# Sparse-attention decode on one Trainium2 core: selected keys on one DMA queue, selected values on the other

## What is computed

```python
# per batch b: 32 pages of 128 past tokens, found through page_table[b]
kc, vc = compressed_kv(dense(pool_cmp_k, kcr), dense(pool_cmp_v, vcr), ...)   # one key and value per 16 tokens
...
p_c = masked_softmax(einsum(q, kc) * sc, mask_c)                # compressed branch
score = where(valid, einsum(p_c.sum(3), overlap) + forced, NEG) # importance of blocks of 64 tokens
top_val, top_idx = top_k(score, 16)
s_s = einsum(q, ks[top_idx]) * sc;  o_s = masked_softmax(s_s) @ vs[top_idx]   # selected branch
o_w = masked_softmax(einsum(q, kw) * sc, mask_w) @ vw                         # last 512 tokens
o = g0 * o_c + g1 * o_s + g2 * o_w
y = x + gate * ((o * silu(z)) @ c_w_out)
# after it, for prompt and sample: y = rmsnorm(y) * final_norm
```

## Time and profile before

| | |
|---|---|
| median of three runs | 1283.19 us (1278.74 to 1287.04) |
| profiled execution, its own time | 1283.88 us |
| its span | 1282.2 us |
| PE busy | 1186.6 us (93%) |
| DVE, ACT, POOL busy | 485.5, 426.2, 200.0 us |
| mean granted clock of TensorE | 0.964 of full speed |
| moved by DMA | 238.77 MB, mean 186 GB/s |

### The profile page before, as it was taken

How to read it: one execution, slowest core, us unless ns; L and a number is a source line. 1 busy time by engine, 2 the same in 40 slices (tenths; PEclk the granted TensorE clock), 3 DMA queues, 4 the chain that set the end, 5 groups by cost and what they waited for, 6 DMA issues and landing times. The chain is left out here.

```text
span 1282.2 us, 25368 instructions
## 1 busy us (share of the span) xinstructions
PE 1186.6 (93%) x9191; PEld 749.0 (58%) x9191; DVE 485.5 (38%) x1491; ACT 426.2 (33%) x1080; POOL 200.0 (16%) x337
## 2 busy tenths in 40 slices
PE   4899999999999799999997999999998979889996
PEld 1677754766767457477875555555554434444455
DVE  2543033444412501022203666556565323333334
ACT  3322113233310420011011656656665223333452
POOL 0000000000000101012002222222223423434300
PEclk8899999999989899999898999999999889989998
DMA  9655543203071302125005767766676989898972
GB/s 382 250 198 197 197 164 91 119 1 132 1 271 66 144 1 73 68 74 186 3 1 207 247 219 260 263 226 224 225 244 193 343 291 310 302 311 283 344 266 75
DMA packets 96440, 238.77 MB, mean 186 GB/s; under 512 B 12602, under 2 KB 50620, under 8 KB 91836
## 3 DMA queue, kind: packets, MB, share of 16 engines
q1 hardware_dynamic: 74076, 169.14, 37.5%
q0 software_dynamic: 22240, 68.02, 15.0%
HBM read 227.57 MB, written 17.05 MB: 191 GB/s over the span
## 5 line engine op out<-in xcount | busy, mean ns | idle before, releaser
L405 PE MATMUL ps<-arena,wring 128*128 128x288 f32 x1664 | 427.3, 413 | 3.7 <-DMA wring<-in_weights 2.2
L405 PEld LDWEIGHTS ps<-arena,wring 128*128 128x128 f32 x1664 | 315.4, 192 | 102.4 <-issue 14.1
L1628 POOL DMA_DIRECT2D arena<-in_cmp_pages x128 | 70.1, 548 | 276.8 <-PE ps L1793 100.5
L414 PE MATMUL ps<-wring,arena 128*128 128x512 f32 x192 | 92.0, 614 | 7.1 <-ACT arena L1366 7.1
L1721 DVE CUSTOM_DVE_ANT_0 wring<-ps,wring 128x128 f32<-128x128 f32 (+3 forms) x128 | 57.6, 488 | 72.4 <-PE ps L1650 71.0
L2186 DVE CUSTOM_DVE_ANT_1 arena<-ps,small 128x512 f32<-128x512 f32 x64 | 44.3, 693 | 93.1 <-PE ps L2105 93.0
L2162 ACT ACTIVATE arena<-arena 128x512 f32<-128x512 f32 (+1 forms) x88 | 57.0, 648 | 67.4 <-DVE arena L2202 67.4
L1713 ACT ACTIVATE wring<-ps 128x128 f32<-128x128 f32 (+3 forms) x128 | 49.1, 436 | 86.8 <-PE ps L1673 86.8
L1699 ACT ACTIVATE wring<-wring 128x128 f32<-128x128 f32 (+3 forms) x128 | 70.7, 559 | 8.6 <-DVE wring L1721 8.5
L2173 ACT ACTIVATE arena<-ps 128x512 f32<-128x512 f32 x72 | 43.0, 598 | 87.0 <-PE ps L2126 87.0
L1786 PE MATMUL ps<-arena 128*32 128x256 f32 x1024 | 69.5, 389 | 0.0
(11 more groups left out here) (396 smaller groups left out, 1572.9 us busy)
## 6 DMA issues: line engine op xcount, KB each, us to landing
wring<-in_weights SPq DMA_DIRECT2D x27, 2048.0 KB, 11.0
arena<-in_cmp_pages SPq DMA_DIRECT2D x128, 256.0 KB, 3.4
arena<-in_cmp_pages POOLq DMA_DIRECT2D x128, 256.0 KB, 4.4
wring<-in_kv_pages SPq DMA_DIRECT2D x64, 256.0 KB, 9.3
wring<-in_kv_pages POOLq DMA_DIRECT2D x64, 256.0 KB, 6.9
arena<-in_kv_pages SPq DMA_DIRECT2D x50, 256.0 KB, 7.3
arena<-in_kv_pages POOLq DMA_DIRECT2D x50, 256.0 KB, 7.1
arena<-in_out_tiles SPq DMA_DIRECT2D x12, 512.0 KB, 7.9
```

What stands on the lines that cost most here:

```text
L405: last = pe.matmul(out[:, 0:HT], w[:, k, ct * P:ct * P + P], moving[k][:, half * HT:half * HT + HT], start=(k == 0), stop=(k == KT - 1))
L414: last = pe.matmul(main, tokens, w[:, k, :], start=(k == 0), stop=(k == KT - 1))
L1628: eng.dma_start(cring[q % CR][:, 2 * half + j, :], v["cmp_pages"][bass.ds(ids[2 * d + j], 1)] .rearrange("o p c -> (o p) c")).then_inc(c_i ...
```

## The change

- **Queues.** SP's queue brings all keys (`load_keys`), GpSimd's all values (`load_values`), one DMA of 128 rows x 256 f32 per page and kind, and one of 512 KB for each half of the window. Each kind has its own semaphores, and a key load waits for the key home alone, a value load for the value home alone. `pe_scores` waits for keys alone; `pe_values` waits for its values. Page numbers are now read per tile and queue, behind the wait, from a table in plain order.
- **Output tiles.** From n = 1 on, output tile n is loaded behind all keys of batch n.
- **Tail.** The samples' last projection is 16 matmuls of 512 columns, from weights in another order (`out_rows`), in four pairs of k that wait for one piece of the weights each. The sum of squares over k is a TENSOR_REDUCE on DVE and one matmul.
- **Prompt's masks.** `prompt_cmp_max(0)` now comes ahead of `prompt_cmp_mask(1)` on DVE.

```diff
@@ names of DV3
-        names = ["ca0", "ca1", "cm0", "cp0"]
+        names = ["ca0", "cm0", "ca1", "cp0"]
...
-        def wait_home(eng, n, i):
+        def load_keys(eng, n, i):
 
             at = n * NL + i
             if at < CR:
...
                 eng.wait_ge(pe_a, PE3["pv", U - 1])
             else:
                 eng.wait_ge(scored, (at - KR) // NL * NJ + (at - KR) % NL + 1)
+            home, done = keys_home(n, i), k_in[at % KR]
+            if i == NG:
+                eng.dma_start(home, v["win_kv"][n, :, 0:HALF]).then_inc(done, 16)
+                return
+            ids = page_ids(eng, 0, (n * NG + i) * GP)
+            for q in range(GP):
+                eng.dma_start(home[:, q * KVW:q * KVW + KVW], v["kv_pages"][bass.ds(ids[q], 1)]
+                              .rearrange("o p c -> (o p) c")[:, 0:KVW]).then_inc(done, 16)
+
+        def load_values(eng, n, i):
+
+            at = n * NL + i
+            if at < CR:
+                eng.wait_ge(pe_c, PC_["pool", NB - 1, CR + 2 + at // 2])
+            elif at < KS:
+                eng.wait_ge(pe_a, PE3["pv", U - 1])
             if KS - CR <= at < KS:
                 eng.wait_ge(dve_c, DC_["sel", NB - 1])
             if at >= KS:
                 n0, i0 = (at - KS) // NL, (at - KS) % NL
                 eng.wait_ge(valued, n0 * NJ + JS.index(i0) + 1)
-
-        def bring(eng, n, i, half, lo, cols, src):
-
-            k, vals, done = keys_home(n, i)[:, lo:lo + cols], values_home(n, i)[:, lo:lo + cols], kv_in[half][(n * NL + i) % KS]
-            if vals.offset > k.offset:
-                both = bass.AP(k.tensor, k.offset, [list(k.ap[0]), [vals.offset - k.offset, 2], [1, cols]])
-                eng.dma_start(both, src.rearrange("p (x c) -> p x c", x=2)).then_inc(done, 16)
-            else:
-                eng.dma_start(k, src[:, 0:cols]).then_inc(done, 16)
-                eng.dma_start(vals, src[:, cols:2 * cols]).then_inc(done, 16)
-
-        def load_kv(eng, half, n, pair):
-            ids = page_ids(eng, 0, ((n * (NG // 2) + pair) * 2 + half) * GP)
-            for d in range(2):
-                i = 2 * pair + d
-                wait_home(eng, n, i)
-                for j in range(2):
-                    bring(eng, n, i, half, (2 * half + j) * KVW, KVW,
-                          v["kv_pages"][bass.ds(ids[2 * d + j], 1)].rearrange("o p c -> (o p) c"))
...
+            home, done = values_home(n, i), v_in[at % KS]
+            if i == NG:
+                eng.dma_start(home, v["win_kv"][n, :, HALF:2 * HALF]).then_inc(done, 16)
+                return
+            ids = page_ids(eng, 0, (n * NG + i) * GP)
+            for q in range(GP):
+                eng.dma_start(home[:, q * KVW:q * KVW + KVW], v["kv_pages"][bass.ds(ids[q], 1)]
+                              .rearrange("o p c -> (o p) c")[:, KVW:2 * KVW]).then_inc(done, 16)
@@ pe_scores
-                pe.wait_ge(kv_in[0][(n * NL + i) % KS], kv_total[0, n, i])
-                if i < NG:
-                    pe.wait_ge(kv_in[1][(n * NL + i) % KS], kv_total[1, n, i])
+                pe.wait_ge(k_in[(n * NL + i) % KR], landed(n, i, KR))
@@ pe_values
+            if j <= NG:
+                pe.wait_ge(v_in[(n * NL + j) % KS], landed(n, j, KS))
@@ SP's program
-                    for pair in range(NG // 2):
-                        load_kv(sp, 0, n, pair)
-                        if pair == 1:
-                            sp.wait_ge(*((tile_done, n) if n else (pe_c, PC_["turn", NB - 1, 1])))
-                            sp.dma_start(lohi_[:, 0:1024], v["out_tiles"][n]).then_inc(tile_in, 16)
-                    load_window(sp, n)
+                    for i in range(NL):
+                        load_keys(sp, n, i)
+                        if n == 0 and i == 3:
+                            sp.wait_ge(pe_c, PC_["turn", NB - 1, 1])
+                            sp.dma_start(lohi_[:, 0:1024], v["out_tiles"][0]).then_inc(tile_in, 16)
+                    if n:
+                        sp.wait_ge(tile_done, n)
+                        sp.dma_start(lohi_[:, 0:1024], v["out_tiles"][n]).then_inc(tile_in, 16)
@@ GpSimd's program
-                    for pair in range(NG // 2):
-                        load_kv(pool, 1, n, pair)
+                    for i in range(NL):
+                        load_values(pool, n, i)
@@ PE, the samples' output projection and the sum of squares
-                for ct in range(4):
-                    for k in range(KT):
+                    for k in range(2 * i, 2 * i + 2):
                         for half in range(2):
-                            last = pe.matmul(ps[half * NS:half * NS + NS, 2 + half, ct * P:ct * P + P], zT[:, k, TP:NT],
-                                             last_w[4 * half + ct][:, k, :], start=(k == 0), stop=(k == KT - 1))
+                            last = pe.matmul(ps[half * NS:half * NS + NS, 2 + half, :], zT[:, k, TP:NT],
+                                             last_w[2 * i + half][:, k % 2, :], start=(k == 0), stop=(k == KT - 1))
...
-                for k in range(KT):
-                    if k == 0:
-                        pe.wait_ge(s_squares, 1)
-                    last = pe.matmul(ps[:, 4, 0:NS], ones, f_sqs[:, k, :], start=(k == 0), stop=(k == KT - 1))
-                last.then_inc(s_summed, 1)
+                pe.wait_ge(s_squares, 1)
+                pe.matmul(ps[:, 4, 0:NS], ones, s_sum, start=True, stop=True).then_inc(s_summed, 1)
@@ DVE
                 prompt_cmp_mask(dve, 0)
+                prompt_cmp_max(dve, 0)
                 prompt_cmp_mask(dve, 1)
-                prompt_cmp_max(dve, 0)
...
-                dve.tensor_tensor(f_sqs, xs, xs, ALU.mult).then_inc(s_squares, 1)
+                dve.tensor_tensor(f_sqs, xs, xs, ALU.mult)
                 dve.drain()
+                dve.tensor_reduce(s_sum, f_sqs.rearrange("p k n -> p n k"), AX.X, ALU.add).then_inc(s_squares, 1)
```

More of the change, by code:

```diff
@@ L217, in out_tiles, with out_rows @@
     return head_pairs(v["c_w_out"][0].T).T.reshape(KT, P, KT, P).transpose(2, 1, 0, 3).reshape(KT, P, KT * P)
+def out_rows(v):
+    return out_tiles(v).reshape(2, 4, P, 4, 2, P).transpose(0, 3, 2, 4, 1, 5).reshape(KT, P, KT * P)
 def narrow_weights(w):
@@ L2026, in build, with landed @@
         sums11 = sums_.rearrange("p (b c) -> p b c", b=2)
-        kv_in = [[sem(f"kv_in_{eng}{s}") for s in range(KS)] for eng in ("sp", "pool")]
-        kv_total, kv_count = {}, [[0] * KS, [0] * KS]
-        for at in range(NB * NL):
-            pieces = 1 if v_homes[at % KS].offset > k_homes[at % KR].offset else 2
-            for h in range(2):
-                kv_count[h][at % KS] += 16 * pieces * (2 if at % NL < NG else 1 - h)
-                kv_total[h, at // NL, at % NL] = kv_count[h][at % KS]
+        k_in = [sem(f"keys_in{s}") for s in range(KR)]
+        v_in = [sem(f"values_in{s}") for s in range(KS)]
+        def landed(n, i, homes):
+            at = n * NL + i
+            return sum(16 * (GP if a % NL < NG else 1) for a in range(at % homes, at + 1, homes))
         JS = list(range(NG)) + [NG + 1, NG]
@@ L2231, in build @@
         f_sqs = SS[:, 0:KT * NS].rearrange("p (k n) -> p k n", k=KT)
-        last_w = [keys_home(NB - 1, 1 + ct).rearrange("p (k c) -> p k c", k=KT) for ct in range(KT)]
-        last_in = [sem(f"last_tiles_in{i}") for i in range(4)]
+        last_w = [keys_home(NB - 1, 1 + i).rearrange("p (k c) -> p k c", k=2) for i in range(KT)]
+        last_in = [sem(f"last_rows_in{i}") for i in range(4)]
         f_squares, f_summed, f_rooted = sem("f_squares"), sem("f_summed"), sem("f_rooted")
@@ L2238, in build @@
         s_tok = SS[:, KT * NS:KT * NS + TP]
+        s_sum = SS[:, KT * NS + TP:KT * NS + TP + NS]
         def pe_out_tile(pe, n):
@@ L2294, in _ @@
                     for h in range(2):
[L2295 removed]
+                        sp.dma_start(keys_home(NB - 1, 1 + 2 * i + h), v["out_rows"][4 * h + i]).then_inc(last_in[i], 16)
                 y = v["y"].rearrange("p (k n) -> p k n", k=KT)
```

10 lines of the change are left out of this document (4 added, 6 removed).

## The result

The changed kernel takes 1273.7 us (median of 20 runs, 1266.85 to 1282.4). The kernel before took 1281.76 us in 20 runs (1276.05 to 1290.24). The ratio is 0.993, 95% interval 0.9908 to 0.9953: faster, but by 6 to 12 us where 24 were forecast. Four stretches hold this difference: 2.1 us lie ahead of 684 us, in code that was not changed (the prompt's first matmuls start anywhere from 680.5 to 690.7 us in the profiled executions of this case); 2.9 us between the prompt's first matmuls and phase 0; 8.0 us in the seven phases; 0.3 us in the tail.

The account below looks back on a forecast made before the run. The prediction took PE to be held up by SP's wait before each output tile, with SP's issuing the next bound. Gains of 3.0 (start), 20 (phases) and 0.9 (tail), 23.9 us, from 1283.9 gave 1260 us; range 1246 to 1281.

Parts of the forecast that it names:

- DMA's pace: Rival for the seven phases: DMA stays at 306 GB/s, 1280.0 us, or reaches 323 GB/s, 1266.7 us; chance 0.30.
- Its second cause: In the phases: window and output tile, issued together, still take 12 us to land and PE waits once a batch; 1280.0 us.
- PE's pace: Rival for the phases: SP's page-number blocks overlap more, so PE bounds; 32.5 us gained there, 1247.5 us in all; chance 0.13.
- SP slower than its own rows: Rival for SP's key loads: 0.75 us a step, so a batch takes 36.2 us and the kernel 1309.5 us; chance 0.12.
- The signs set down: Trace signs of being right, among them phases 1 to 6 at 29 to 30 us each and 330 to 345 GB/s.
- the chance of 0.68: Chance of a time under 1270.4 us, faster by more than 1% (13 us); within 1% had 0.20, slower 0.12.
- 29.2 us of issuing per batch: SP's queue in the phases: eight tiles of 3.52 us plus window and output tile, more than PE's 27.9 us.
- I allow one such stall per batch in six, 0.5 us a batch: SP's loads in the phases: allowance for a full queue holding a load 2.74 us; lowers the gain from 22.9 to 20 us.
- the 7.9 us of the earlier trace: Start of phase 1: time from output tile 1's issue to its landing, putting that phase's start at 1039.6 us.
- The start: Prompt's first masks on DVE: DVE goes on 3.1 us earlier and PE takes it all, 3.0 us gained.
- The tail: End of the kernel: wide matmuls gain nothing, the sum of squares on DVE brings the reciprocal earlier; 0.9 us gained.
- put at nothing: GpSimd's value loads in the phases: 28.1 us per batch, costed at nothing because its lead of over 25 us covers it.

Follow-up runs that it names:

- e1: Changed kernel with SP taking the keys' page numbers as program constants instead of reading them from the table; 1248.64 us, ratio 0.9763 to the kernel before.
- e2: Changed kernel with loads of 128 x 128 instead of 128 x 256 on both queues from the seventeenth tile on, same instructions; 1269.89 us, ratio 0.9907.
- e7: Changed kernel without the range checks of page numbers on both queues, loads still dynamic; 1251.56 us, ratio 0.9779 to the kernel before.
- e9: Changed kernel without the split (each queue brings keys and values of its pages) and without bound checks of page numbers; 1252.65 us, ratio 0.9791.
- e4: Kernel before with only the first masks' order, the wide projection matmuls and the sum of squares on DVE changed; 1281.04 us, ratio 0.9983.
- e3: Kernel before with only output tile n (n from 1) moved behind the window of batch n; 1258.66 us, ratio 0.9825.
- e10: Changed kernel with key loads of 16 rows instead of 128 after the first round of homes; 1262.27 us (one run).
- e11: Changed kernel with value loads of 16 rows instead of 128 after the first round of homes; 1260.13 us (one run).

## Why the prediction was off

- **What bounds the changed kernel: right.** SP's wait for PE is gone, SP's issuing sets the pace (e1, e2, e7), PE's waits end with the keys, the window and the output tile, and values cost nothing. Rival "DMA's pace" would have explained the time (1266.7 to 1280) and the share of 1.00, but e1, e2 and e7 refute its mechanism for the pace. Its second cause is seen in part: the output tile takes 10 us to land, and PE waits for it in five phases, 3.3 us in all. "PE's pace" is what comes once SP is relieved, at 1247.5 by the forecast and 1248.64 to 1252.65 in e1, e7 and e9. "SP slower than its own rows" is wrong in its form: the median load takes 0.33 us and steps of 0.52. The signs set down were met only in part: of phases 1 to 6 three take 29.4 to 30.2 us and three 31.8 to 32.6, at 307 to 335 GB/s. And the chance of 0.68 was for a time under 1270.4 us; 1273.7 lies in the part within 1%, which had 0.20. That it lies in the range of 1246 to 1281 us is owed to the width that "DMA's pace" gave the range, a mechanism that isn't the cause.
- **The step that failed: the size of SP's batch**, in "29.2 us of issuing per batch" and "I allow one such stall per batch in six, 0.5 us a batch". The rows had it right for an undisturbed batch (28.5 by the shortest steps). The stretch of single issues was 2.5 us a batch, not 0.5, with 0.3 of waits beside it, and it is not the stall of a full queue by which I priced it (2.74 us): it is there at 187 GB/s too. SP was 31.3 us a batch against 29.7. From phase 1 to phase 7 six batches took 1224.74 - 1038.54 = 186.2 us against 6 x 29.7 = 178.2: **8.0 us**.
- **Landing of the output tile**: the 7.9 us of the earlier trace rows were misread. The trace of before has no landing for the eight output tiles of the phases; the median is that of four loads of the last weights, issued from 1226.8 to 1230.2 us. An output tile behind SP's wait landed in 3.3 us (median in e4, whose phases have the same program). Now it leaves right behind the window's keys and lands in 10.0 (7.2 in e2 with half the bytes). Batch 1's window left 22.9 us after the start of phase 0 instead of 21.2. Phase 0 took 33.6 instead of 29.7 us: **3.9 us**. With the 8.0 above that is the 11.9 us by which the phases missed (219.8 against 204.9 + 3.0).
- **The range of this step.** I took 32.5 us (PE's pace) and nothing as its bounds; e3 shows where the value was to be looked for. The move of the tile is worth 22 to 23 us alone, near PE's pace, and the split takes 11 to 14 us of it back by doubling SP's page-number blocks (8 for 4 of 1.6 us) and its issues. The prediction summed both into one batch of 29.2 us and so never put a price on the split, the one part that was a loss.
- **The start: right.** 3.4 us against 3.0.
- **The tail**: 0.3 us against 0.9. The reduce takes 1.01 us, not 0.7: half of the elements cost more than half of the time, for which no run shows the reason (it sums groups of 8, the one it was priced by takes the maximum of groups of 32). The last projection took 9.4 us, before 8.9, but its granted clock was 0.75 against 0.81. At 2.4 GHz throughout both would need 7.0 to 7.2 us (an estimate from these figures), so that no cost of the wide matmuls is shown.
- **GpSimd**: 31.2 us a batch, not 28.1 (1.36 us and at times 1.65 for page numbers instead of 1.13, and 0.59 us a step of its loads). It stays free in this kernel, as its lead of a phase covers it: no wait for values at L2147. That it was put at nothing is right only as long as SP is as slow; in e1 it costs 2.5 us in the last phase.

Of the 23.9 us forecast, then, 11.9 are missing in the phases and 0.6 in the tail, and 0.4 more came at the start. The sum leaves 11.8 us. The profiled execution shows 11.2 from 684 us on, as 0.5 of the 3.4 us at the start are gone by phase 0; its 2.1 us ahead of 684 us are scatter. The medians of 20 runs give 8.1 us.

## What to carry to other kernels

Add up what an issuing queue needs for one period of its loop, its register work included, and compare it with the period of the engine it feeds. Taking the wait out of the queue with slack (19 us of issuing in 27.9) brought the kernel near PE's pace and gained 22 us; in the queue without slack the same move gained 4 to 7, and any edit that gives the full queue more instructions is paid for in each period. A DMA share near 1.0 does not show that the DMA is the bound; a run with half the bytes and the same instructions tells whether it is. When a bound goes, look for the next: here GpSimd's 31.2 us a batch was hidden by a lead that lasts for eight batches. Price each part of a change on its own, with a sum for each, since a good part can hide a bad one (here 23 us won and 11 lost).

## What the runs showed of the hardware

- A dynamic page number costs SP more than the DMA that uses it: 1.56 to 1.60 us for four with range checks against four issues of 0.33 us. The checks (152 + 18 ns each, four a tile, with their gaps) were about 1 us of it. Without them on both queues the kernel is some 19 us faster (e7 against the changed kernel, 0.9779 against 0.993).
- The DMA share is no measure of what is left: it read 1.00 at 326 GB/s and 1.06 at 358 GB/s with the same kind of loads.
- Single issues on SP take 1 to 1.7 us where the median is 0.33, with half the bytes and with few rows too, and up to 5 us for loads of 2 x 256 (e9, 353 GB/s). With an emptier DMA they nearly always come right behind a 16 KB packet of the instruction queue (35 of 37 in e2, e10 and e11). GpSimd's issues stay within 0.06 us of their median in the same runs.
